# Norm, residual and norm before and after a feed forward: whole width or two halves of 256 tokens

## The chip, the core and the metric

The kernel is one program on one core of one Trainium2 chip. Its engines are TensorE (PE; weight loads are PEld), VectorE (DVE), ScalarE (ACT), GpSimd (POOL) and SyncE (SP, which issues DMAs). They run their own instruction streams in order and meet only at semaphores. The metric is the device time of one execution in microseconds (us), lower is better.

## The reference, cut to what matters

Two transformer-like blocks work on 512 tokens of width 1024. What the change touches is the end of the first block and the start of the second:

```python
def rmsnorm(x, g):
    ms = jnp.mean(xf * xf, axis=-1, keepdims=True)
    return (xf * lax.rsqrt(ms + EPS) * g)
...
    h = h + rmsnorm(mixed @ w_out[l], g_mix_post[l])      # border 1, first norm and residual
    hn = rmsnorm(h, g_ffn_pre[l])                         # border 1, second norm
    f = jnp.square(jax.nn.relu(hn @ w_ff1[l])) @ w_ff2[l] # the feed forward
    h = h + rmsnorm(f, g_ffn_post[l])                     # border 2, first norm and residual
...
    h = rmsnorm_2(x, norm1_g[l]) * (1.0 + sc1) + sh1      # border 2, second norm
    z = h @ w_in[l]                                       # conv_in ("cin"), latents, gates
```

Everything is float32 and each token is normed by itself, so a border can be done for some tokens ahead of the others.

## The kernel before, in words

Activations lie transposed: the partition is a channel and the free dimension holds the tokens, so a tile of width 1024 is 8 rows of 128x512. A matmul with float32 accuracy is made of three float32r ones: operands are split into a high part (an ACT copy that rounds) and a low part (a subtraction), and `three` (line 338) multiplies high by high, high by low and low by high. Weights are streamed in units of 128x2048 through a ring. For each unit ACT writes the high part (`high`, line 821) and DVE or POOL the low part (`low`, line 1339) into one of two places of `wsplit`; `high` of a unit waits until the unit two before it is used up. The order of units is the list PLAN, written out by hand; POOL_LOW says whose low part is POOL's. `next_high` and `next_low` handle the unit after the one named.

`linear` (line 346) does one unit: two output tiles of 128x512, each 8 rows of the input by three matmuls, 24 in all, into one of 8 PSUM banks. Units in the order of the program: "wo" 0 to 3 (w_out, tiles 0 to 7), then "f1" 0 to 7 and "f2" 8 units, twice over, with "ada" units between them that DVE alone works on, then "cin" 0 to 3, "lat", "ga", "gc" and so on. An f2 tile sums over two units.

A border is done across all 512 tokens:

- while the last linear units run, ACT squares each output row (`block_out`, line 1051, or line 1109) and DVE sums the squares in `nrm[:, 2]` (`sums`, line 1679). PE sums over the partitions with a matmul by ones (`total`), ACT takes the root (line 847), DVE the reciprocal (line 1369) into `rs`.
- `residual` (line 1689): for each of 8 rows DVE multiplies by gain and rs (line 1697), and DVE (even rows, line 1701) or POOL (odd rows, line 2227) adds it to X. ACT squares each row of X (`squares_of_x`, line 1063), PE sums the squares with eight matmuls by ones; then again root and reciprocal.
- for each row DVE makes the value (line 1713, in border 2 line 1778), ACT the high part (line 1082, in border 2 line 1118, and for odd rows line 1120), DVE (even rows, lines 1719 and 1782) or POOL (odd rows, lines 2234 and 2239) the low part. `linear("f1", i, ..., each="h_split")` follows row by row.

After border 1, for each f1 tile ACT takes ReLU and square (lines 1094 and 1096), DVE the square again and the low part (lines 1756 and 1759), and DVE adds an ada unit into `adab` (line 1735) ahead of the next unit's low part. After border 2, tiles cin 0 to 3 are copied to `CA` and 4 to 7 go through a sigmoid (`conv_gate`). A causal convolution of 31 taps on DVE (`convolve`, lines 1796 and 1799) starts when cin tiles 4 and 5 are there.

## Time and profile before

| what | value |
|---|---|
| median of 3 runs | 2111.68 us (2108.8 to 2114.98) |
| the profiled execution's own time | 2114.34 us |
| its span in the profile | 2112.5 us |
| mean granted TensorE clock | 0.925 of 2.4 GHz |
| PE / DVE / ACT / POOL busy | 88% / 63% / 37% / 23% |

The profile gives for each engine what it was busy with and what ended the idle time before it. In a row of the timeline the first number is the start from the span's start, the second the duration (of all of the instructions, where several are merged); the arrow in brackets names what the engine had waited for.

### The profile page before, as it was taken

Reading aid. Unit: us, or ns where it says so; the run is one execution under the profiler, and the core shown is the slowest. Engines: PE = TensorE matmul, PEld = TensorE weight load, DVE = VectorE, ACT = ScalarE, POOL = GpSimd, SP = SyncE. Lnnn points to the kernel's source line nnn. Section 1 sums busy time; section 2 is a strip of 40 time slices with the busy share of each in tenths; the row PEclk is TensorE's granted clock in tenths of the full one; section 3 lists DMA queues with packets and bytes.
Section 4 is the critical chain, followed back from the end, with each engine's and each line's share of the span. In section 5 each row is a group of like instructions: output and inputs, shape, how many; then the busy total and the mean of one; then the engine's idle time right before and its main releaser. Section 6 shows DMA issues by size and latency. Waiting matters only on the chain. (4 is left out here: it accounts for less than half of the span.)

```text
span 2112.5 us, 21287 instructions
## 1 busy us (share of the span) xinstructions
PE 1849.6 (88%) x8780; PEld 1447.2 (69%) x8780; DVE 1330.5 (63%) x1664; ACT 779.2 (37%) x994; POOL 496.4 (23%) x417
## 2 busy tenths in 40 slices
PE   4999878789699999699999996998688897789985
PEld 3778756677697888477888784776554574677774
DVE  3235588879545343566235455798978565798995
ACT  3343334332003123343123223324246433666663
POOL 1030066767242000110000001433200000544440
PEclk8999887789899999899999997999889998899997
DMA  6121020002001223134334341221110111989893
GB/s 224 62 80 61 20 80 0 1 21 85 16 2 60 80 100 126 54 140 163 148 147 180 140 159 41 85 100 60 60 60 1 40 40 48 358 341 349 338 352 148
DMA packets 37329, 241.35 MB, mean 114 GB/s; under 512 B 4192, under 2 KB 4704, under 8 KB 10736
## 3 DMA queue, kind: packets, MB, share of 16 engines
q1 hardware_dynamic: 23984, 147.69, 18.9%
q0 software_dynamic: 13248, 92.30, 11.4%
q8 instruction: 69, 1.13, 0.2%
q14 instruction: 28, 0.23, 0.0%
HBM read 228.39 MB, written 11.58 MB: 114 GB/s over the span
## 5 line engine op out<-in xcount | busy, mean ns | idle before, releaser
L336 PE MATMUL bank<-h_high,wsplit 128*128 128x512 f32 x992 | 323.4, 405 | 25.6 <-POOL wsplit L1339 8.6
L1339 DVE TENSOR_TENSOR wsplit<-ring,wsplit 128x2048 fp32r<-128x2048 f32 x77 | 177.4, 2304 | 182.0 <-ACT wsplit L821 181.9
L821 ACT ACTIVATE wsplit<-ring 128x2048 fp32r<-128x2048 f32 x98 | 186.9, 1907 | 212.3 <-PE bank L336 188.3
L336 PEld LDWEIGHTS bank<-h_high,wsplit 128*128 128x128 f32 x992 | 190.3, 192 | 79.9 <-POOL wsplit L1339 9.5
L336 PE MATMUL bank<-xn_high,wsplit 128*128 128x512 f32 (+1 forms) x832 | 219.9, 352 | 27.0 <-DVE wal_low L1390 18.5
L336 PE MATMUL bank<-h_low,wsplit 128*128 128x512 f32 x496 | 199.5, 402 | 0.0
L336 PEld LDWEIGHTS bank<-xn_high,wsplit 128*128 128x128 f32 x832 | 148.3, 194 | 49.3 <-issue 19.9
L336 PE MATMUL bank<-f_high,wsplit 128*128 128x512 f32 x512 | 166.3, 405 | 4.4 <-DVE f_low L1759 4.4
L2227 POOL TENSOR_TENSOR x<-x,z 128x512 f32<-128x512 f32 x8 | 12.8, 1594 | 598.8 <-DVE z L1697 598.8
L336 PE MATMUL bank<-xn_low,wsplit 128*128 128x512 f32 (+1 forms) x416 | 145.6, 350 | 0.0
L1799 DVE SCALAR_TENSOR_TENSOR conv<-conv_in,vecs,conv 128x512 f32<-128x512 f32 x120 | 140.5, 1171 | 4.3
L2263 POOL DMA_INDIRECT ring<-in_wmoe,indices x42 | 84.1, 2002 | 219.7 <-DVE routing L1999 139.8
L1339 POOL TENSOR_TENSOR wsplit<-ring,wsplit 128x2048 fp32r<-128x2048 f32 x21 | 98.3, 4682 | 113.0 <-ACT wsplit L821 112.7
L336 PEld LDWEIGHTS bank<-f_high,wsplit 128*128 128x128 f32 x512 | 99.3, 194 | 29.3 <-DVE f_low L1759 5.2
L336 PEld LDWEIGHTS bank<-h_low,wsplit 128*128 128x128 f32 x496 | 95.6, 193 | 22.2 <-issue 0.2
L336 PE MATMUL bank<-states,d_re 128*32 128x64 f32 x512 | 91.3, 294 | 18.1 <-DVE states L1618 18.1
L336 PE MATMUL bank<-f_low,wsplit 128*128 128x512 f32 x256 | 103.7, 405 | 0.0
L336 PE MATMUL bank<-states,d_im 128*32 128x64 f32 x512 | 91.7, 295 | 0.0
L336 PE MATMUL bank<-parts,block_high 128*128 128x512 f32 x216 | 74.1, 426 | 18.4 <-DVE block_out L2081 18.4
L336 PEld LDWEIGHTS bank<-xn_low,wsplit 128*128 128x128 f32 x416 | 80.7, 194 | 10.8 <-issue 0.7
L336 PE MATMUL bank<-m_high,wsplit 128*128 128x512 f32 x256 | 81.3, 396 | 2.0 <-DVE m_low L1928 2.0
L336 PE MATMUL bank<-g_high,wsplit 128*128 128x512 f32 x256 | 80.8, 395 | 0.0
(465 smaller groups left out, 3890.2 us busy)
## 6 DMA issues: line engine op xcount, KB each, us to landing
ring<-in_W SPq DMA_DIRECT2D x122, 1024.0 KB, 4.8
xslot<-zeros SPq DMA_DIRECT2D x7, 516.0 KB, 5.0
block<-xslot SPq DMA_DIRECT2D x7, 516.0 KB, 11.0
yslot<-block_out SPq DMA_DIRECT2D x7, 512.0 KB
x_in<-in_xT SPq DMA_DIRECT2D x4, 528.0 KB, 7.4
x<-in_xT SPq DMA_DIRECT2D x2, 1024.0 KB, 6.2
out_y<-h_tokens SPq DMA_DIRECT2D x4, 512.0 KB, 2.6
bc<-in_bc SPq DMA_DIRECT2D x1, 1024.0 KB, 4.7
```

Of the source, the lines that this page charges most:

```text
L336: return g.matmul(o, l, r, start=first, stop=last_, skip_group_check=True)
L821: g.activation(wst[:, side(n), 0, :], ringt[:, n % RING, :], ACT.Copy).then_inc(*a.sig(("high", n)))
L1339: g.tensor_tensor(wst[:, side(n), 1, :], ringt[:, n % RING, :], hi, SUB).then_inc(*t.sig(("low", n), ("released", n)))
L1799: g.scalar_tensor_tensor(out=CO[:, c, :], in0=i, scalar=cw[:, c, k:k + 1], in1=CO[:, c, :], op0=MUL, op1=ADD).then_inc(*v.sig(("convolved",)))
L2227: g.tensor_tensor(X[:, k, :], X[:, k, :], Z[:, k, :], ADD).then_inc(*q.sig((name, "x", k)))
L2263: g.indirect_dma_start(slots[c % NS], None, wmoe, indexed(x)).then_inc(slot_landed[c % NS], 16)
```

## The change

Both borders are done for the tokens 0 to 255 (half 0) and then 256 to 511 (half 1).

- PE: the last unit before a border (wo 3, f2 15; f2 14 too) is done as four half tiles of 24 matmuls with 256 columns, in the order (6, half 0), (7, half 0), (6, half 1), then the ones matmuls that sum half 0's squares, then (7, half 1). Then the eight ones matmuls for X of half 0, the sum for half 1's first norm, and the first two units after the border (f1 0 and 1, cin 0 and 1) as four tiles for half 0 and four for half 1. The ones matmuls for X of half 1 stand between the rows of the fourth half tile.
- DVE and POOL share the rows otherwise: DVE does both operations of rows 0, 2, 4, 6 and 7, POOL both of rows 1, 3 and 5. For POOL's rows ACT multiplies by the gain beforehand (`pool_rows`). DVE's sum of squares ends at row 5; rows 6 and 7 go to ones matmuls of their own.
- ACT: between the second root of half 0 and half 0's high parts stand the squares of half 1's last tiles, `pool_rows`, the high part of the next weight unit and the first root of half 1.
- DVE: the low part of that weight unit stands between half 0 and half 1. The low part of cin 1 is now DVE's and no longer POOL's. In border 2 the last sums of half 1 (`last_sum(1)`) stand behind the residual of half 0.
- High parts of f1 2 and cin 2 stand behind what ACT does with all eight half tiles.
- The load of positions waits for all of border 2 (`h2_done`).

```diff
-POOL_LOW = {... + [("cin", i) for i in (1, 2, 3)]
+POOL_LOW = {... + [("cin", i) for i in (2, 3)]
...
+        HALF = (slice(0, 256), slice(256, 512))
+        DVE_ROWS, POOL_ROWS, ROWS_COME = (0, 2, 4, 6, 7), (1, 3, 5), (0, 1, 2, 3, 4, 6, 5, 7)
... PE
+            def tile_half(name, i, j, h, xh, xl, need, beside=None):
+                n = UNIT[name, i]
+                wh, wl = weights(n, 8, 2048)
+                m, c = slice(128 * j, 128 * j + 128), HALF[h]
+                p.wait_ge(*at("low", n))
+                b = fresh(name, 2 * i + j, h)[:, 0:256]
+                for s, k in enumerate(ROWS_COME):
+                    p.wait_ge(*at(*need(k, h)))
+                    t = three(b, wh[:, k, m], wl[:, k, m], xh[:, k, c], xl[:, k, c], s == 0, s == 7)
+                    if beside and s < 7:
+                        beside(s)
+                t.then_inc(*p.sig((name, 2 * i + j, h), ("used", n)))
...
+            def mean_square(after, name, h):
+                b = fresh(after, h)[:, 0:256]
+                p.wait_ge(*at(name + "_added", 5))
+                mm(b, ones, nrm[:, 2, HALF[h]], True, False)
+                for z in range(2):
+                    p.wait_ge(*at(name + "_square", 6 + z, h))
+                    t = mm(b, ones, nrm[:, z, HALF[h]], False, z == 1)
...
+            def border(after, name, pre, first, xh, xl, need):
+                for s in range(8):
+                    square_of_x(pre, 0, s)
+                mean_square(after, name, 1)
+                for j in range(4):
+                    tile_half(first, j // 2, j % 2, 0, xh, xl, need, (lambda s: square_of_x(pre, 1, s)) if j == 3 else None)
+                for j in range(4):
+                    tile_half(first, j // 2, j % 2, 1, xh, xl, need)
...
+            for j, h in ((0, 0), (1, 0), (0, 1)):
+                tile_half("wo", 3, j, h, mh, ml, split)
+            mean_square("mix_post", "wo", 0)
+            tile_half("wo", 3, 1, 1, mh, ml, split)
+            border("mix_post", "wo", "ffn_pre", "f1", hh, hl, lambda k, h: ("h_split", k, h))
... ACT
+            next_high("wo", 3)
+            root_table()
+            last_tiles(0)
+            half_root("mix_post", 0)
+            squares_of_x("ffn_pre", 0)
+            half_root("ffn_pre", 0)
+            last_tiles(1)
+            pool_rows("ffn_pre", Z, vec("g_ffn_pre"), 0)
+            next_high("f1", 0)
+            half_root("mix_post", 1)
+            h_high(0)
+            squares_of_x("ffn_pre", 1)
+            half_root("ffn_pre", 1)
+            pool_rows("ffn_pre", Z, vec("g_ffn_pre"), 1)
+            h_high(1)
+            g.activation(cact, vec("c_2"), ACT.Sigmoid).then_inc(*a.sig(("c_sig",)))
+            for h in range(2):
+                for j in range(4):
+                    ... ReLU and square of f1 tile j, half h, 256 columns each
+            next_high("f1", 1)
... DVE
+            def residual(name, after, gain, out, h):
+                v.wait_ge(*at("root", after, h))
+                g.reciprocal(rs[:, c], rs[:, c]).then_inc(*v.sig(("inverse", after, h)))
+                for k in DVE_ROWS:
+                    g.scalar_tensor_tensor(out=Z[:, k, c], in0=Z[:, k, c], scalar=gain[:, k:k + 1], in1=rs[:, c], op0=MUL, op1=MUL).then_inc(*v.sig())
+                    v.wait_ge(*v.own())
+                    g.tensor_tensor(X[:, k, c], X[:, k, c], Z[:, k, c], ADD).then_inc(*v.sig((name, "x", k, h)))
+            residual("ffn_pre", "mix_post", vec("g_mix_post"), "wo_out", 0)
+            scaled_half("ffn_pre", Z, vec("g_ffn_pre"), "h_value", "h_split", 0, h_low)
+            next_low("f1", 0)
+            residual("ffn_pre", "mix_post", vec("g_mix_post"), "wo_out", 1)
+            scaled_half("ffn_pre", Z, vec("g_ffn_pre"), "h_value", "h_split", 1, h_low)
...
+                    if hf == 0 and i == 0:
+                        ... low parts of f1 tiles 0 to 3, half 0 then half 1, 256 columns each
+                    elif hf == 0 and i == 1:
+                        pass
... POOL
+                for k in POOL_ROWS:
+                    g.tensor_tensor(Z[:, k, c], Z[:, k, c], rs[:, c], MUL).then_inc(*q.sig())
+                    q.wait_ge(*q.own())
+                    g.tensor_tensor(X[:, k, c], X[:, k, c], Z[:, k, c], ADD).then_inc(*q.sig((name, "x", k, h)))
... ACT, behind border 2
+            for h in range(2):
+                for j in range(4):
+                    a.wait_ge(*at("cin", j, h))
+                    g.activation(CA[:, j, HALF[h]], banks.at("cin", j, h)[:, 0:256], ACT.Copy).then_inc(*a.sig(("free", "cin", j, h), ("cin_out", j)))
             conv_gate(1)
... SP
-            s.wait_ge(*at("h2_split", 6))
+            s.wait_ge(*at("h2_done"))
```

Border 2 is written in the same way with "ffn_post", "attn_pre", cin, `h2_high` (Identity with a bias, and a second one for rows 1, 3 and 5) and `h2_low`.

## Rows read from the trace of the kernel before

**Rows 1.** The page's first part, busy time and share of the span.

```profile
PE 1849.6 (88%) x8780; PEld 1447.2 (69%) x8780; DVE 1330.5 (63%) x1664; ACT 779.2 (37%) x994; POOL 496.4 (23%) x417
```

**Rows 2.** Stretches: bounds, length, busy (x) of PE, PEld, DVE, ACT, POOL, clock, DMA.

```profile
870.70:899.10 28.40, 10.82 (x19) 3.38 (x18) 20.49 (x19) 10.15 (x16) 6.38 (x4) 0.74 0.00 0
899.10:904.50 5.40, 5.15 (x10) 3.11 (x11) 5.40 (x7) 1.95 (x4) 3.48 (x2) 0.50 0.00 2
...
920.00:1260.00 340.00, 335.62 (x1445) 270.69 (x1444) 159.00 (x123) 96.43 (x102) 0.00 (x0) 0.98 0.42 158
```

**Rows 3.** Timeline, border 1, from the last wo matmul to the residual.

```profile
870.33 0.40 PE L336 MATMUL bank<-m_high,wsplit 128*128 128x512 f32 x1
...
873.02 1.13 PE L336 MATMUL bank<-norm_tmp,cst 128*128 128x512 f32 x2 [2.30 <-DVE norm_tmp L1685]
...
874.19 0.69 ACT L847 ACTIVATE norm_tmp<-bank,cst 128x512 f32<-128x512 f32 x1 [0.59 <-PE bank L336]
874.98 3.35 DVE L1369 RECIPROCAL norm_tmp<-norm_tmp 128x512 f32<-128x512 f32 x1 [2.10 <-ACT norm_tmp L847]
...
879.83 1.41 DVE L1697 SCALAR_TENSOR_TENSOR z<-z,vecs,norm_tmp 128x512 f32<-128x512 f32 x2
...
880.65 1.70 POOL L2227 TENSOR_TENSOR x<-x,z 128x512 f32<-128x512 f32 x1 [204.22 <-DVE z L1697]
...
881.27 1.64 DVE L1701 TENSOR_TENSOR x<-x,z 128x512 f32<-128x512 f32 x1
...
889.64 1.26 POOL L2227 TENSOR_TENSOR x<-x,z 128x512 f32<-128x512 f32 x1 [1.29 <-DVE z L1697]
```

**Rows 4.** Groups by tile: durations min/median/max in ns of the border's 512-column instructions.

```profile
L1701 DVE TENSOR_TENSOR x<-x,z x8: 691/1636/1640, 879.2 to 1302.8; 128x512 f32<-128x512 f32 x8
L1118 ACT ACTIVATE h_high<-h,adat x8: 722/724/727, 1313.3 to 1323.2; 128x512 fp32r<-128x512 f32 x8
```

**Rows 5.** Timeline behind border 1: DVE's ada and low part, ACT's ReLU of tiles 2, 3.

```profile
918.01 2.35 DVE L1735 SCALAR_TENSOR_TENSOR ada_sum<-ring,small,ada_sum 128x2048 f32<-128x2048 f32 x1
920.27 2.28 DVE L1339 TENSOR_TENSOR wsplit<-ring,wsplit 128x2048 fp32r<-128x2048 f32 x1
...
921.64 0.60 ACT L1094 ACTIVATE norm_tmp<-bank 128x512 f32<-128x512 f32 x1 [2.53 <-PE bank L336]
927.24 0.60 ACT L1094 ACTIVATE norm_tmp<-bank 128x512 f32<-128x512 f32 x1 [4.33 <-PE bank L336]
```

**Rows 6.** Timeline, border 2: last f2 matmul, POOL's low part, ACT's copy of cin 3, next high part.

```profile
1286.11 0.40 PE L336 MATMUL bank<-f_high,wsplit 128*128 128x512 f32 x1
...
1328.04 4.87 POOL L1339 TENSOR_TENSOR wsplit<-ring,wsplit 128x2048 fp32r<-128x2048 f32 x1 [1.82 <-ACT wsplit L821]
...
1344.47 0.60 ACT L1128 ACTIVATE conv<-bank 128x512 f32<-128x512 f32 x1 [5.00 <-PE bank L336]
1348.57 1.90 ACT L821 ACTIVATE wsplit<-ring 128x2048 fp32r<-128x2048 f32 x1
```

**Rows 7.** The chain that ended last, behind border 2: start, length, what.

```profile
1332.97 22.68 PE bank L336 x96
```

**Rows 8.** Half-size relatives elsewhere in the kernel: durations min/median/max in ns.

```profile
L1305 ACT ACTIVATE hidden<-bank x28: 385/385/388, 1821.5 to 2082.5; 128x256 f32<-128x256 f32 x28
L2071 DVE TENSOR_TENSOR hidden<-hidden,bank x28: 420/420/423, 1822.9 to 2083.3; 128x256 f32<-128x256 f32 x28
L1353 POOL TENSOR_TENSOR pool_products<-powers,bc x48: 702/748/1150, 291.4 to 622.4; 128x288 f32<-128x288 f32 x48
```

**Rows 9.** Timeline, matmuls with 264 columns, first and last of 26 like them.

```profile
45.03 0.28 PE L336 MATMUL bank<-xn_low,wsplit 128*128 128x264 f32 x1
...
54.15 0.29 PE L336 MATMUL bank<-xn_low,wsplit 128*128 128x264 f32 x1
```

**Rows 10.** Timeline, DVE and POOL working beside each other on 288 columns.

```profile
290.86 1.72 DVE L1357 TENSOR_TENSOR d_re<-products 64x288 f32<-64x288 f32 x2
...
292.35 1.90 POOL L1357 TENSOR_TENSOR d_re<-pool_products 64x288 f32<-64x288 f32 x2
```

More of the change, by code:

```diff
@@ L604, in tensor, with total @@
             p.end("end", "ffn", "pe")
-            total("ffn_post", nrm[:, 2, :], ("ffn_squares",))
-            squares_of_x("attn_pre")
+            border("ffn_post", "ffn", "attn_pre", "cin", hh2, hl2, lambda k, h: ("h2_split", k, h))
             hb = [(0, hh2, hl2)]
-            for i in range(4):
-                linear("cin", i, hb, each="h2_split")
+            for i in range(2, 4):
+                linear("cin", i, hb)
+            def total(name, a, *need):
+                b = fresh(name)
+                for w in need:
+                    p.wait_ge(*at(*w))
+                mm(b, ones, a, True, True).then_inc(*p.sig((name,)))
+                banks.close(name)
             for i in range(3):
@@ L1051, in block_out, with pool_rows @@
+            def pool_rows(name, to, gain, h):
+                c = HALF[h]
+                for k in POOL_ROWS:
+                    a.wait_ge(*at(name, "x", k, h))
+                    g.activation(to[:, k, c], X[:, k, c], ACT.Copy, scale=gain[:, k:k + 1]).then_inc(*a.sig((name, "gained", k, h)))
+            a.wait_ge(*at("end", "glu", "pe"))
+            a.wait_ge(*at("end", "glu", "dve"))
+            for i in range(3):
+                next_high("wo", i)
                 for j in (2 * i, 2 * i + 1):
-                    a.wait_ge(*at(name, j, 0))
@@ L1076, in scalar @@
-            root_table()
-            root(("mix_post",), rs, 1024, 512)
-            squares_of_x("ffn_pre")
-            a.wait_ge(*at("end", "wo", "pe"))
-            for k in range(8):
-                a.wait_ge(*at("h_value", k))
-                g.activation(hh[:, k, :], Z[:, k, :], ACT.Copy).then_inc(*a.sig(("h_high", k)))
-            g.activation(cact, vec("c_2"), ACT.Sigmoid).then_inc(*a.sig(("c_sig",)))
+                        a.wait_ge(*at("wo_added", j - 2))
+                    b = banks.at("wo", j, 0)
@@ L1084, in scalar @@
+            next_high("f1", 1)
             for hf in range(2):
-                for i in range(8):
+                for i in range(0 if hf else 2, 8):
                     next_high("f1", 8 * hf + i)
@@ new lines, in scaled_half @@
+            def scaled_half(name, o, gain, value, split, h, low_of):
+                c = HALF[h]
+                v.wait_ge(*at("root", name, h))
+                g.reciprocal(rs[:, c], rs[:, c]).then_inc(*v.sig(("inverse", name, h)))
+                v.wait_ge(*v.own())
+                g.scalar_tensor_tensor(out=o[:, 0, c], in0=X[:, 0, c], scalar=gain[:, 0:1], in1=rs[:, c], op0=MUL, op1=MUL).then_inc(*v.sig((value, 0, h)))
+                for k, after in zip(DVE_ROWS, DVE_ROWS[1:] + (None,)):
+                    if after:
+                        g.scalar_tensor_tensor(out=o[:, after, c], in0=X[:, after, c], scalar=gain[:, after:after + 1], in1=rs[:, c],
+                                               op0=MUL, op1=MUL).then_inc(*v.sig((value, after, h)))
+                    low_of(k, c, split, h)
@@ new lines, in scaled_half, with value_of @@
+            def scaled_half(name, o, hi, lo, value, high_, split, h):
+                c = HALF[h]
+                def value_of(k):
+                    q.wait_ge(*at("inverse", name, h))
+                    q.wait_ge(*at(name, "gained", k, h))
+                    q.wait_ge(*q.own())
+                    g.tensor_tensor(o[:, k, c], o[:, k, c], rs[:, c], MUL).then_inc(*q.sig((value, k, h)))
+                value_of(POOL_ROWS[0])
+                for k, after in zip(POOL_ROWS, POOL_ROWS[1:] + (None,)):
+                    if after:
+                        value_of(after)
+                    q.wait_ge(*at(high_, k, h))
+                    q.wait_ge(*q.own())
+                    g.tensor_tensor(lo[:, k, c], o[:, k, c], hi[:, k, c].bitcast(F32), SUB).then_inc(*q.sig((split, k, h)))
```

266 lines of the change are left out of this document (158 added, 108 removed).

## The prediction

> **What bounds the kernel now.** I read the busy shares first: PE is busy 88% of the span, more than any other engine [rows 1], so time is lost where PE stands. The view by stretches shows two such places, alike. Between the feed forward's ends PE works 335.6 of 340 us, so nothing is to be gained there; in border 1 it works only 10.8 of 28.4 us, on the ones matmuls of the norms, and then 5.4 us at a granted clock of 0.50, 1.2 of 2.4 GHz, behind the splits [rows 2]. The timeline says what goes on meanwhile: a reciprocal of 3.35 us, twice, and rows that DVE and POOL pass between them [rows 3]. Counted to a full rate, border 1 costs this: wo's last matmul ends at 870.7, tiles 2 and 3 are 5.6 us apart, and f1 tile 3 ends at 927.2 [rows 3, 5]; that is 56.5 us for four tiles of 5.6, so 34 are lost. Border 2 runs from 1286.5 to cin tile 3 at 1344.4 [rows 6], 57.9 us, 35.5 lost. What comes behind hangs on PE in both cases: behind border 1 the feed forward, behind border 2 the chain goes through four PE tiles, 96 matmuls [rows 7], to DVE's convolution. So what counts is when unit f1 2, and when unit cin 2, can begin. Before, f1 2 begins at 927.2 and cin 2 at 1344.4.
>
> I count from the start of the last unit before a border, two tiles of 5.6 us ahead of its end: 859.5 and 1275.3. On that clock f1 2 begins at 67.7 and cin 2 at 69.1.
>
> **Prices at half width.** A matmul with 264 columns comes every 0.1216 us (75 in 9.12) [rows 9], so 256 columns take 0.118 and a half tile of 24 takes 2.83, half a full one: PE pays nothing for halving. ACT takes 0.385 from a bank [rows 8]; the step from 512 to 256 columns is 0.21, from 0.60 [rows 6]. So an Identity goes from 0.724 to 0.51 and a root from 0.69 to 0.48 [rows 3, 4]; copies and squares from memory lie between, I take 0.42. DVE pays 0.42 for a tensor-tensor [rows 8] against 0.69 [rows 4] and 0.70 for its products [rows 3], so two halves cost 0.15 more than the whole each time; with the gap to the next I take 0.45. A reciprocal halves to about 1.75. A ones matmul goes from 1.13 to 0.57 [rows 3]. POOL takes 0.70 for 288 columns and 1.26 for 512 [rows 3, 8], so 0.62 for 256.
>
> The price that decides is that of DVE and POOL together. DVE's addition takes 0.69 at best but 1.64 in the median [rows 4], POOL's 1.26 alone and 1.70 beside DVE [rows 3]. In the timeline POOL's ends 1.11 us behind DVE's product (881.24 to 882.35), and DVE's addition 0.56 behind POOL's end (882.91) [rows 3]: they take turns, and only their starts overlap. For 288 columns beside each other DVE needs 0.86 and POOL 0.95 for one [rows 10], about 0.9 a pair; for 256 I take 0.8. The ends of this price: 0 for the wait, when DVE alone sets the pace, and the full sum of 0.45 and 0.62, 1.07. The row with 288 columns is the nearest, so it decides.
>
> One phase (residual, or value and split) has ten DVE and six POOL instructions: the first DVE one 0.5, six pairs 4.8, three DVE ones left 1.4, together **6.7 us** for a half. Before, the residual of all 8 rows ran from the reciprocal's end at 878.3 to POOL's last addition at 890.9, 12.6 us [rows 3]; twice 6.7 is 13.4. Halving thus makes the border's own work longer; it is the cover by PE that must pay.
>
> The Trainium skill, SBUF — State Buffer, Who interferes with whom, speaks against this more strongly: there the later of the two blocks until the other's whole instruction is over. The rows above show a shorter exclusion. By its rule the sum below would lie about 11 us higher.
>
> **Border 1, step by step.** Three half tiles 8.5; three ones matmuls 1.7 (10.2); root 0.5 (10.7); reciprocal 1.75 (12.45); residual of half 0 6.7 (19.15); last square, ones matmul, root 1.5 (20.65). Now ACT, not DVE, is late: four operations on the last tiles 1.6, three gains 1.3, the high part of f1 1 1.9 [rows 6], root 0.5, and the first high part 0.4 (26.4), while DVE's reciprocal is done at 22.4. Then DVE has eight instructions left and POOL four: four pairs 3.2 and four alone 1.8 (31.4). Half 1 follows: low part of f1 1 2.3 [rows 5] (33.7), reciprocal 1.75, residual 6.7 (42.15), square, ones, root 1.5, reciprocal 1.75 (45.4), values and splits 6.7 (52.1), last row's matmuls 0.4 (52.5), three half tiles 8.5 (61.0). The four tiles of half 0 lie inside (31.8 to 43). Here a **new wait** opens: the high part of f1 2 no longer runs beside the tiles, it stands behind all eight ReLUs, and DVE has an ada unit before its low part. ReLU and square 0.9, DVE's low part of the tile 0.4, ada 2.35, low part 2.3 [rows 5]: f1 2 begins at 67.0. ACT's backlog of half 0 tiles (from 52.5, with the sigmoid's table) is gone by about 60, just in time. Against 67.7 the gain is **0.7 us**.
>
> The moved sums of squares cost nothing on the path; they hide beside the half tiles of the last unit, and without that cover would cost 0.4 to 0.7 each.
>
> **Border 2.** The same to 20.65; ACT's part is squares 0.85, gains 1.3, high part 1.9, root 0.5 (25.2), then eleven Identities of 0.51 (30.8) and the last low 0.5 (31.3), so ACT binds there. `last_sum(1)` on DVE (0.85) lies beside ACT's squares. Then 2.3, 1.75, 6.7, 1.5, 1.75 and 6.7 (52.0), 0.4 and 8.5 (60.9). Behind it stand the copy of tile 3 (0.4), the high part of cin 2 (1.9) and POOL's low part at 4.87 [rows 6], less 0.1 when nothing contends: cin 2 begins at 68.0 against 69.1, gain **1.1 us**. Taking cin 1's low part from POOL spares nothing more; before, it ended at 1332.91 just ahead of the tiles that needed it, at 1332.97 [rows 6, 7], and ahead of the convolution. The position load is later, but DVE then has over 10 us until tiles 4 and 5 for it. SP's weight loads move with the use of their units and have one ring of lead.
>
> Sum: 0.7 + 1.1 = 1.8 us off. Of the profiled execution, 2114.34 us (span 2112.5), that leaves 2112.5; the median of the runs lies 2.7 lower, so I forecast **2109.9 us**. 0.3%, 6.3 us, is about what a measurement of this kernel can tell from no change.
>
> **Rivals.**
> - *The two engines overlap more than taken.* If DVE's own pace (4.7 a phase) sets it, border 1 gains three times 2.0 and 1.4, border 2 three times 2.0: 13.4 more, 2096.5. For: POOL has fewer, shorter instructions, and DVE runs one-input work too. Against: [rows 10]. Chance 0.22.
> - *PE's half clock falls on the path* (the other side). Behind border 1 PE ran 5.4 us at 0.50, after an idle stretch, where ten matmuls of 512 columns filled 5.15 us [rows 2]; before, that was hidden behind the splits. Now three tiles of half 1 stand behind the last split, with nothing beside them. At half clock a 256-column matmul streams 256 / 1.2 GHz = 0.213, so each takes 5.1 instead of 2.83: 7 us a border, 14 in all, 2123.9. It decides as soon as more than 3 us a border are slow. For: an idle of about 3 us before half 1's splits, and row-wise matmuls that fill PE partly. Against: behind border 1 such row-wise matmuls brought the clock back, for the ReLUs of tiles 2 and 3 are 5.6 us apart [rows 5]. Chance 0.12. The Trainium skill, TensorE: Matmul & The Clock Gate, What's actually happening, has the same rule, that the array is throttled by default and activity releases it.
> - *Turns by whole instructions.* A pair costs 1.07 instead of 0.8: 22 pairs in border 1 and 18 in border 2 on the path, 10.8 us more, 2120.7. For: medians of 1.64 and 1.70. Against: the 0.56 and 1.11 above. Chance 0.08. This is the SBUF page's rule of the Trainium skill.
> - *A wait not seen*, in a program with so many new semaphores: 0.05.
>
> **How the numbers follow.** The forecast case has 0.53 and its own range is 2104 to 2117, from handoffs of 0.04 us (sum's end at 874.15 to the root at 874.19 [rows 3]) at some twenty steps a border and 0.1 a pair either way. About 0.05 of it falls under 2105.4 and 0.03 over 2118. Faster: 0.22 + 0.05 = 0.27; slower: 0.12 + 0.05 of the third rival + 0.03 of the last + 0.03 of the case = 0.23; within 0.3%: 0.50. The range reaches most of the way to both sides: 2098 to 2122.
>
> **What would show it.** In the profile after, residual and value phases of about 6.7 us with DVE and POOL in turns; about 4 us between the second reciprocal of half 0 and its first low part, with ACT busy; PE idle for about 6 us between the last half tile and f1 2, and 7 before cin 2; the feed forward between unchanged. I'd be wrong if phases took 5 us or 8, if the half 1 tiles took over 3 us each, if f1 2 began well ahead of its place, or if the convolution did not move with cin 2.

## The result, and the profile after

The changed kernel takes **2122.1 us** (median of 5, 2121.0 to 2124.1) where the kernel before took 2113.4 beside it: a ratio of 1.0041 [1.0027, 1.0056]. It is slower by 9 us, and in later runs again: 1.0060 [1.0045, 1.0075]. The forecast was 2109.9, a small gain. The profiled execution took 2122.0 us with a span of 2120.2, 7.7 more than before.

Four marks that both kernels have cut the span into comparable pieces: ACT's first read of wo tile 5 (the last unit before border 1 starts there), ACT's ReLU of f1 tile 4 (the first tile of unit f1 2), DVE's last modulation sum (just ahead of border 2), and ACT's sigmoid of cin tile 5 (the last of unit cin 2). A modulation sum is what follows a group of ada units, three times in the feed forward: PE sums `adab` over the partitions with sixteen matmuls of one output column each, and DVE adds the result into `adat`. The timeline of the kernel before, by start, length, engine and what ended the idle time ahead of it:

```profile
859.56 0.60 ACT L1053 ACTIVATE z<-bank 128x512 f32<-128x512 f32 x1 [4.28 <-PE bank L336]
...
932.84 0.60 ACT L1094 ACTIVATE norm_tmp<-bank 128x512 f32<-128x512 f32 x1 [2.53 <-PE bank L336]
...
1273.85 0.17 DVE L1742 TENSOR_TENSOR adat<-bank,vecs 128x16 f32<-128x16 f32 x1 [8.11 <-PE bank L336]
...
1355.67 0.60 ACT L1131 ACTIVATE conv_in<-bank 128x512 f32<-128x512 f32 x1 [3.29 <-PE bank L336]
```

The same four of the changed kernel:

```profile
859.52 0.60 ACT L1144 ACTIVATE norm_tmp<-bank 128x512 f32<-128x512 f32 x1 [4.51 <-PE bank L339]
...
935.57 0.60 ACT L1200 ACTIVATE norm_tmp<-bank 128x512 f32<-128x512 f32 x1 [3.31 <-PE bank L339]
...
1279.37 0.17 DVE L1887 TENSOR_TENSOR adat<-bank,vecs 128x16 f32<-128x16 f32 x1 [9.27 <-PE bank L339]
...
1367.07 0.60 ACT L1262 ACTIVATE conv_in<-bank 128x512 f32<-128x512 f32 x1 [5.00 <-PE bank L339]
```

So border 1 takes 76.05 us instead of 73.28 (+2.8), the feed forward behind it 343.8 instead of 341.0 (+2.8), border 2 87.7 instead of 81.8 (+5.9); behind it 3.7 come back (753.1 against 756.8), which makes the 7.7.

The waits that the prediction announced are there. PE's waits from 871 to 928 and from 1291 to 1354 (what ended them; us in total, times, longest):

```profile
PE bank L339 <- DVE h_low L1848: 8.5, 2, 4.6
PE bank L339 <- DVE wsplit L1471: 5.9, 1, 5.9
...
PE bank L339 <- DVE h_low L1852: 8.2, 2, 4.7
PE bank L339 <- POOL wsplit L1471: 6.9, 1, 6.9
```

5.9 us for DVE's low part of f1 2 and 6.9 for POOL's of cin 2. The chain that ended last goes through them, from half 1's last tiles to the convolution:

```profile
1333.49 12.65 PE bank L339 x87
...
1346.16 0.38 ACT conv L1267
1346.54 1.81 ACT wsplit L882
...
1348.48 4.51 POOL wsplit L1471
...
1353.04 14.01 PE bank L339 x48
```

The last line is the surprise: 48 matmuls are two tiles, 11.2 us at full rate, and they take 14.0. The view by stretches says why (bounds, length, PE busy, granted clock, DMA share, GB/s). Border 1, where [rows 2] had its stretches before:

```profile
871.00:899.00 28.00, 20.75 (x119) 0.88 0.00 1
899.00:905.00 6.00, 4.46 (x28) 1.00 0.00 0
905.00:913.00 8.00, 4.81 (x23) 0.79 0.01 2
913.00:922.00 9.00, 8.87 (x75) 1.00 0.59 233
922.00:928.00 6.00, 0.21 (x1) 0.76 0.23 66
928.00:940.00 12.00, 12.00 (x44) 0.83 0.83 318
```

and border 2:

```profile
1291.00:1312.00 21.00, 14.38 (x64) 0.81 0.00 0
...
1335.00:1346.00 11.00, 11.00 (x82) 0.86 0.38 121
1346.00:1353.00 7.00, 0.12 (x2) 0.67 0.00 0
1353.00:1359.00 6.00, 5.96 (x15) 0.53 0.49 175
```

While PE stands for the weights of f1 2 or cin 2, the granted clock falls toward 0.50, 1.2 of 2.4 GHz, and the tile behind the wait starts there: 0.53 over 1353 to 1359. Before, nothing stood at these places: f1 2's high part ran beside the tiles, and ACT read f1 2's first tile 5.6 us behind the last of f1 1 (927.24 in [rows 5], 932.84 in the first list above).

### The profile page after: what moved, and what is told of

The parts are those of the page before. It is cut to its first block, busy times and chain, and to the rows that moved or that the text cites. A ratio compares the mean times of both kernels' runs of the same rounds, so it can differ in the third digit from the quotient of the medians.

```text
span 2120.2 us, 22234 instructions
## 1 busy us (share of the span) xinstructions
PE 1862.0 (88%) x9168; PEld 1489.4 (70%) x9168; DVE 1333.0 (63%) x1707; ACT 792.5 (37%) x1065; POOL 505.1 (24%) x448
## 4 chain that ended last, share of the span: by engine, by line
PE 65%; DVE 26%; ACT 5%; issue 3%; DMA 1%; POOL 1%; SPq 0%; POOLq 0%; DVEq 0%; ACTq 0%
PE bank L339 64%; DVE conv L1961 7%; DVE u_shuffled L1722 2%; DVE states L1750 1%; DVE products L1745 1%; DVE wsplit L1471 1%; DVE states L1748 1%; DVE wsplit L2209 1%; DVE products L1746 1%; DVE parts L2209 1%; DVE qk L1501 1%; DVE norm_tmp L1501 1%; ACT wsplit L882 1%; ACT parts L1414 1%; ACT probs_t L1333 0%
## 5 line engine op out<-in xcount | busy, mean ns | idle before, releaser
L339 PE MATMUL bank<-h_high,wsplit 128*128 128x512 f32 (+1 forms) x1120 | 342.6, 388 | 39.3 <-POOL wsplit L1471 15.1
L339 PEld LDWEIGHTS bank<-h_high,wsplit 128*128 128x128 f32 x1120 | 215.1, 199 | 85.2 <-POOL wsplit L1471 15.7
L339 PE MATMUL bank<-h_low,wsplit 128*128 128x512 f32 (+1 forms) x560 | 214.0, 382 | 0.0
L339 PE MATMUL bank<-f_high,wsplit 128*128 128x512 f32 (+1 forms) x576 | 170.2, 381 | 4.4 <-DVE f_low L1924 4.4
L2393 POOL TENSOR_TENSOR z<-z,norm_tmp 128x256 f32<-128x256 f32 x12 | 9.2, 767 | 586.1 <-DVE norm_tmp L1824 585.2
L2444 POOL DMA_INDIRECT ring<-in_wmoe,indices x42 | 85.5, 2036 | 218.9 <-DVE routing L2161 136.4
L339 PEld LDWEIGHTS bank<-h_low,wsplit 128*128 128x128 f32 x560 | 112.1, 200 | 20.7 <-issue 0.2
L339 PEld LDWEIGHTS bank<-f_high,wsplit 128*128 128x128 f32 x576 | 107.9, 195 | 26.4 <-DVE f_low L1924 5.2
L1471 POOL TENSOR_TENSOR wsplit<-ring,wsplit 128x2048 fp32r<-128x2048 f32 x20 | 93.7, 4686 | 120.7 <-ACT wsplit L882 120.3
L339 PE MATMUL bank<-f_low,wsplit 128*128 128x512 f32 (+1 forms) x288 | 109.3, 380 | 0.0
L339 PE MATMUL bank<-parts,block_high 128*128 128x512 f32 x216 | 73.8, 425 | 18.4 <-DVE block_out L2243 18.4
L339 PE MATMUL bank<-m_high,wsplit 128*128 128x512 f32 (+1 forms) x288 | 83.1, 372 | 2.0 <-DVE m_low L2090 2.0
```

Of the source, the lines that this page charges most:

```text
L339: return g.matmul(o, l, r, start=first, stop=last_, skip_group_check=True)
L1471: g.tensor_tensor(wst[:, side(n), 1, :], ringt[:, n % RING, :], hi, SUB).then_inc(*t.sig(("low", n), ("released", n)))
L2444: g.indirect_dma_start(slots[c % NS], None, wmoe, indexed(x)).then_inc(slot_landed[c % NS], 16)
```

## The experiments

Each kernel was timed against the kernel before on the same chip. **Theory A**, from the profile: the halves work as forecast, and each border loses by its new wait and by PE's half clock behind it. **Theory B**: the halves themselves (shorter instructions, fixed costs, turns of DVE and POOL) cost it. Measured, in the pieces above (wo 5 to f1 4, f1 4 to the last modulation sum, that to cin 5, the rest of the span), from the one profiled execution of each:

| kernel | ratio to before, 95% | border 1 | feed forward | border 2 | rest |
|---|---|---|---|---|---|
| before | 1 | 73.3 | 341.0 | 81.8 | 756.8 |
| changed | 1.0041 [1.0027, 1.0056] | 76.1 | 343.8 | 87.7 | 753.1 |
| after_again | 1.0060 [1.0045, 1.0075] | 76.2 | 343.7 | 87.8 | 753.2 |
| b1only | 1.0025 [1.0015, 1.0035] | 76.2 | 343.4 | 82.6 | 751.6 |
| warm | 1.0024 [1.0011, 1.0038] | 74.2 | 342.1 | 85.5 | 751.8 |
| warm_all | 1.0026 [1.0014, 1.0037] | 74.2 | 342.2 | 84.4 | 753.2 |
| warm_more | 1.0013 [1.0003, 1.0023] | 74.2 | 342.2 | 83.0 | 757.7 |
| ada_warm | 1.0038 [1.0025, 1.0052] | 76.0 | 343.9 | 84.4 | 753.1 |
| before_warm | 0.9995 [0.9984, 1.0005] | 73.2 | 338.1 | 84.1 | 753.7 |
| early_f1 | 1.0011 [0.9998, 1.0024] | 70.3 | 342.1 | 87.9 | 753.4 |
| early_cin | 1.0004 [0.9991, 1.0016] | 76.1 | 343.8 | 78.0 | 754.7 |
| early_both | 0.9993 [0.9982, 1.0004] | 71.9 | 343.0 | 78.5 | 755.7 |
| mid_high | 0.9959 [0.9945, 0.9972] | 71.3 | 340.0 | 78.2 | 757.0 |
| mid_high2 | 0.9956 [0.9941, 0.9971] | 70.0 | 338.5 | 78.1 | 753.6 |
| best | 0.9980 [0.9968, 0.9992] | 70.2 | 341.3 | 77.2 | 751.7 |
| best2 | 0.9976 [0.9966, 0.9986] | 71.6 | 339.9 | 78.2 | 759.5 |
| best_warm | 0.9956 [0.9938, 0.9974] | 69.3 | 339.4 | 74.1 | 753.7 |
| mid_high_warm | 0.9946 [0.9932, 0.9961] | 69.2 | 343.7 | 76.1 | 754.7 |

Besides changed and after_again, two pairs are the same code (mid_high and mid_high2, best and best2): their borders differ by up to 1.5 us and their rest by up to 7.8. A difference of the rest is therefore not read as an effect, and one of 1.5 us in a single border only where several kernels repeat it: the five that keep the changed border 1 agree there to 0.2 us (76.0 to 76.2), and the three warm ones to 0.1 (74.2).

### Is it the clock behind the waits? (warm)

Nothing is moved; matmuls whose sums nobody reads are put into PE's two waits.

```diff
+            def warm(name, x, now, then, n):
+                b = fresh(name)
+                for k in range(now):
+                    mm(b, x[:, 0:128], x, True, True)
+                p.wait_ge(*at("high", n))
+                for k in range(then):
+                    t = mm(b, x[:, 0:128], x, True, True)
...
+                        if hf == 0 and i == 2:
+                            warm("warm1", hh[:, 0, :], 8, 8, UNIT["f1", 2])
...
+            warm("warm2", hh2[:, 0, :], 8, 10, UNIT["cin", 2])
             for i in range(2, 4):
                 linear("cin", i, hb)
```

> Matmuls whose sums nobody reads are put into PE's two new waits of the changed kernel: 8 of 512 columns right behind the last half tile of f1 0/1 and 8 more behind the high part of f1 2, and 8 and 10 in the same places before cin 2. All waits stay. Theory A (each wait costs its length of 6 and 7 us, and then PE's half clock costs again, for the first tile behind the wait takes 7.8 and 8.4 us where a tile takes 5.6): f1 2 and cin 2 begin where they do in the changed kernel, 927.7 and 1353.0 on its clock, but their first tiles take about 5.6 us; 2.2 + 2.8 = 5.0 us less than the changed kernel, about 2117. Theory B (the phases of DVE and POOL at half width are what costs; PE's clock behind the wait is hidden or chance): no change, 2122, within 1 us. If the added matmuls run at half clock themselves they take 6.9 and 7.7 us, end up to 1 us late, and the gain shrinks to 3.

It took 1.9 us off border 1 and 2.2 off border 2; the ratio of 1.0024 stands against 1.0041 and 1.0060 of the changed kernel. That is 4.1 us where 5.0 were expected, in the direction that only theory A allows. Part of what is missing is in the expectation: at the full clock the first tile behind such a wait takes 5.9 us from its first matmul to ACT's read (929.09 to 934.99 and 1351.09 to 1356.99 in warm), not 5.6, so of the 7.8 and 8.4 us of the changed kernel 1.9 and 2.5 are the clock's. The stretches of the kernel warm over its two waits and the tiles behind them:

```profile
922.00:928.00 6.00, 5.13 (x26) 1.00 0.16 59
928.00:934.00 6.00, 4.92 (x22) 1.00 0.92 352
...
1345.00:1351.00 6.00, 3.53 (x15) 1.00 0.00 0
1351.00:1357.00 6.00, 5.91 (x25) 1.00 0.49 175
```

1.00 throughout, where the changed kernel had 0.76 and 0.83, 0.67 and 0.53. From ACT's read of the last half tile to the first matmul of f1 2 are 5.88 us, 5.89 in the changed kernel; only the clock differs. The unread matmuls did not fill the wait for cin 2 to its end:

```profile
1351.09 0.50 PE L339 MATMUL bank<-h_high,wsplit 128*128 128x512 f32 x1 [2.14 <-POOL wsplit L1484]
```

### Take the waits away (early_f1, early_cin, early_both)

```diff
             for h in range(2):
+                if h:
+                    next_high("f1", 1)
                 for j in range(4):
...
-            next_high("f1", 1)
...
+                            if h:
+                                ada_begin(UNIT["f1", 1] + 1)
+                                next_low("f1", 1)
```

> Border 1 alone: ACT makes the high part of f1 2 ahead of half 1's ReLUs, and DVE the ada unit and the low part of f1 2 ahead of half 1's low parts. The side of the split weights is free when f1 0 has its half 1 tiles, two half tiles (5.7 us) before f1 1 ends; high 1.9 and low 2.3 are 4.2, so they fit. Theory A: the wait of 6 us before f1 2 is gone, f1 2 begins at 921.8 to 922.5 instead of 927.7, and its first tile takes 5.6 to 6 instead of 7.8: 5.2 + 2.0 = 7.2 to 8.1 us less than the changed kernel, some of it given back at the ada matmuls, about 2115. Theory B (halving itself costs it, the handoffs behind the border are as good as hidden): less than 2 us less, since PE would then find another wait in the feed forward, 2120 or more.

Border 1 fell by 5.7 us, to 70.3, with a ratio of 1.0011. The expectation of 7.2 to 8.1 was too high for a reason that the profile shows: f1 2's weights were not there, and ACT stood 2.5 us for their transfer with half 1's ReLUs behind it. Their place in the ring is that of a modulation unit, which DVE reads only behind half 1's splits. The timeline of mid_high, which has the same order there (DVE frees the place at 914.8, SP's transfers start, and the high part can start at 919.64):

```profile
913.54 1.29 DVE L1877 TENSOR_SCALAR ada_sum<-ring,small 128x2048 f32<-128x2048 f32 x1
...
914.86 17.02 SPq L2476 DMA_DIRECT2D ring<-in_W  x6
...
919.64 1.92 ACT L882 ACTIVATE wsplit<-ring 128x2048 fp32r<-128x2048 f32 x1 [2.35 <-DMA ring<-in_W]
```

The same for border 2:

```diff
-POOL_LOW = {UNIT[p] for p in [("zg", i) for i in range(4)] + [("zs", 0), ("zs", 1)] + [("cin", i) for i in (2, 3)]
+POOL_LOW = {UNIT[p] for p in [("zg", i) for i in range(4)] + [("zs", 0), ("zs", 1)] + [("cin", 3)]
...
+                    if h and j == 2:
+                        next_high("cin", 1)
                     a.wait_ge(*at("cin", j, h))
...
             g.tensor_scalar(PR, PR, PI_IN, -PI_IN, ALU.min, MAX).then_inc(*v.sig(("angles",)))
+            next_low("cin", 1)
```

> Border 2 alone: the high part of cin 2 is made between half 1's second and third copies, and its low part on DVE (2.3 us) behind the position angles instead of on POOL (4.5). High at 1340.3 to 1342.2, DVE's angles end at 1342.8, low until 1345.1, the last half tile ends at 1346.1 on the changed kernel's clock. Theory A: cin 2 begins at 1346.1 instead of 1353.0 and its first tile takes 5.6 instead of 8.4: DVE's convolution moves up by 6.9 + 2.8 = 9.7 us; behind it up to a third is given back, as the 11 us lost in the changed kernel shrank to about 8: 2113 to 2115. Theory B: the tiles of half 1 are the loss and a wait ahead of the sigmoid's part stays: under 3 us, 2119 or more.

Border 2 took 78.0, 9.7 under the changed kernel, just as expected, and the kernel is level with the one before (1.0004). ACT makes the high part between two copies, DVE the low part behind the angles, and both are done before the last half tile:

```profile
1339.03 1.91 ACT L882 ACTIVATE wsplit<-ring 128x2048 fp32r<-128x2048 f32 x1
...
1341.00 2.29 DVE L1470 TENSOR_TENSOR wsplit<-ring,wsplit 128x2048 fp32r<-128x2048 f32 x1
...
1344.43 0.39 ACT L1267 ACTIVATE conv<-bank 128x256 f32<-128x256 f32 x1 [2.45 <-PE bank L339]
```

Both together:

> The early splits of f1 2 and of cin 2 together, without those of f1 1 and cin 1. Alone they took 0.30% and 0.37% off the changed kernel (1.0011 and 1.0004 against 1.0041). If the two borders add: 0.67%, a ratio of 0.9974, 5.5 us under the kernel before. Theory B (the halves themselves cost what the changed kernel lost): it cannot go below 1.0000, as a border of two halves would be no shorter than before. What mid_high had beyond this, 0.9959 against 0.9974, is then the worth of the first units' early splits: 3 us, not the 6 hoped for.

71.9 and 78.5 in the borders, within 1.6 and 0.5 us of their own runs. The ratio, 0.9993 [0.9982, 1.0004], misses the 0.9974 expected, so it doesn't refute theory B by itself. The borders speak against it: both are shorter than the whole ones before (73.3, 81.8), border 2 by 3.3 us, which is more than two profiles of one program differ by, border 1 by 1.4, which is not. What refutes it is mid_high, below.

### One border alone, and the changed kernel again (b1only, after_again)

b1only takes the changed code for border 1 and the kernel before for border 2, line for line.

> The change at border 1 alone; border 2 and the units beside it as in the kernel before. In the changed kernel the high parts of the middle of the feed forward are 2.7 us late, and the last modulation sum ahead of border 2 is 5.5 us late. Theory A (each border loses by its own new wait and the clock behind it): 2.7 to 5.5 us above the kernel before, a ratio of 1.0013 to 1.0026, and border 2 takes as long as it did. Theory C (the loss is one of border 2, the late start in the feed forward is made up): under 1 us, a ratio of 1.0005 or less. Theory D (the shift of 2.8 us between 1156 and 1279 in the changed kernel was chance of the clock): the shift at 1279 is 2.7 us, not 5.5.

> The changed kernel, unaltered, beside the others on this chip, so that their ratios to the kernel before stand beside its own. Every theory: the ratio of 1.0041 again, within 0.0015.

1.0025 [1.0015, 1.0035], 5.3 us, inside what theory A said: in the profile border 1 costs 2.9 in itself and 2.4 in the feed forward, and border 2 takes 82.6, nearly what it did (81.8). So theory C (a loss of border 2 alone) falls, and theory D too, as the longer feed forward comes with border 1's code. Every kernel with border 1 and the feed forward unaltered has 343.4 to 343.8 there. after_again lies 0.0019 above 1.0041, where 0.0015 was expected at most; the two intervals overlap, so the loss is known as 0.4 to 0.6%.

### What the halves cost with the clock kept up (warm_all, warm_more, before_warm)

warm_all puts unread matmuls also before the half tiles of each half:

```diff
                 mean_square(after, name, 1)
+                warm(pre + "_warm0", wst[:, side(n0), 0, 0:512], (("high", n0), 0), (("root", pre, 0), 8), ((value, 0, 0), 4))
                 for j in range(4):
                     tile_half(first, ...)
+                warm(pre + "_warm1", wst[:, side(n0), 0, 0:512], (("root", pre, 1), 8), ((value, 0, 1), 4))
```

> The changed kernel with unread matmuls in all six waits of the two borders: those of the kernel warm (in front of f1 2 and cin 2), and 8 of 512 columns behind the second root of each half, 4 more behind its first value, so that PE does not stand before the half tiles either. Theory A: in border 2 of the changed kernel the half tiles of half 0 held up the ones matmuls (1.4 us) and the half tiles of half 1 ran at 0.63 to 0.68 for 10 us; both gone, border 2 from the last modulation sum to cin tile 5 takes 87.7 - 2.8 - 1.4 - 1.5 = 82 us, and border 1 (73.3 us before, 76.1 changed, 74.2 in warm) takes 73.5 to 74; the whole 3 us under warm, a ratio of 1.0010. Theory B: no less than warm, 1.0024 or more.

A miss: 84.4 in border 2, not 82, and 1.0026, which by itself is what theory B said (1.0024 or more). Half 1's last tile indeed ended 2.4 us sooner behind the first root (52.6 us, 1286.80 to 1339.35, against 54.9), but PE stood 2.13 us before cin 2, and the clock was 0.65 from 1348 to 1352:

```profile
1341.58 2.58 PE L339 MATMUL bank<-h_high 128*128 128x512 f32 x10 [0.43 <-ACT wsplit L898]
1346.30 0.49 PE L339 MATMUL bank<-h_high,wsplit 128*128 128x512 f32 x1 [2.13 <-POOL wsplit L1487]
```

The kernel warm had the same gap of 2.14 us and 1.00 behind it, so the gap alone doesn't decide; what else does, no run here shows. warm_more bridges it:

```diff
-                            warm("warm1", hh[:, 0, :], (None, 8), (("high", UNIT["f1", 2]), 8))
+                            warm("warm1", hh[:, 0, :], (None, 8), (("high", UNIT["f1", 2]), 12))
...
-            warm("warm2", hh2[:, 0, :], (None, 8), (("high", UNIT["cin", 2]), 10))
+            warm("warm2", hh2[:, 0, :], (None, 8), (("high", UNIT["cin", 2]), 18))
```

> warm_all with 12 instead of 8 unread matmuls behind the high part of f1 2 and 18 instead of 10 behind that of cin 2, so that PE works until POOL's low part ends. In warm_all border 2, from the last modulation sum to cin tile 5, took 84.4 us and its first tile behind the wait 1.5 us more than 5.6. Theory A: 82.9 us here (81.8 in the kernel before), border 1 as in warm_all (74.2 against 73.3); the ratio 1.0018 where warm_all had 1.0026. What is left, 0.9 and 1.1 us, is the halves' own price, not the clock's.

83.0 and 74.2, and 1.0013. With the clock at 1.00 through the tiles of half 1 and of cin 2, the two borders cost 0.9 and 1.1 us more than whole rows. So by these profiles 6.6 of the 8.7 us lost in the two borders go with the clock; the 2.1 left are the halves together with their two new waits, which still stand here. The 1.1 is no larger than the spread of border 2 (81.8 and 82.6 for the same code, in before and b1only); the 0.9 repeats in all three warm kernels.

before_warm puts them into the kernel before, behind the sums of squares of each border:

```diff
             squares_of_x("ffn_pre")
+            warm("warm1", wst[:, side(n0), 0, 0:512], (("high", n0), 8), (("root", "ffn_pre"), 8), (("h_value", 0), 6))
```

> The kernel before with unread matmuls in the two waits behind the squares (8, 8 and 6 of 512 columns). If the half clock was hidden there behind the splits, as the forecast had it: f1 tile 2 and cin tile 2 begin no sooner, border 1 takes 73.3 and border 2 81.8 us as before, ratio 1.0000 within 0.0010. If it was not hidden: 1 to 3 us less a border, 0.9975.

The clock did rise. The stretch 896 to 904, before and in before_warm:

```profile
896.00:904.00 8.00, 4.65 (x10) 0.50 0.00 1
...
896.00:904.00 8.00, 5.32 (x18) 1.00 0.00 1
```

So it did from 1312 to 1322 (0.50 before, 1.00 here). Yet the ratio is 0.9995 and border 1 73.2: before, the half clock cost nothing in border 1. In the two pieces behind it, the last modulation sum came 2.9 us sooner and border 2 took 84.1, 2.3 more than expected; their sum is the same to 0.6 (422.2 against 422.8).

### The feed forward (ada_warm)

The stretches around the second and third modulation sum, before:

```profile
1152.00:1160.00 8.00, 8.00 (x31) 0.79 0.62 235
1272.00:1280.00 8.00, 8.00 (x36) 0.79 0.32 117
```

and in the changed kernel:

```profile
1152.00:1160.00 8.00, 8.00 (x39) 0.61 0.11 27
1276.00:1284.00 8.00, 8.00 (x44) 0.57 0.13 36
```

PE works without a pause there, but on matmuls of one column, and the clock falls behind them, in both kernels and for longer in the changed one. The whole 2.8 us of the feed forward arise at these two places: from f1 tile 4 to the first sum both kernels take 91.4 us, from there to the second 128.3 and 129.5, to the third 121.3 and 122.9. ada_warm puts an unread matmul of 512 columns behind every fourth of them.

```diff
                         for j in range(16):
                             t = mm(b[:, j:j + 1], adab[:, 128 * j:128 * j + 128], ones[:, 0:1], True, True)
+                            if j % 4 == 3:
+                                u = mm(w, fh[:, 0, 0:128], fh[:, 0, :], True, True)
```

> The changed kernel with an unread matmul of 512 columns behind every fourth of the sixteen one-column matmuls of each modulation sum, 12 in all, which cost 2.8 us by themselves. In the changed kernel PE is granted 0.50 for some 4 to 6 us behind each of the three sums. Theory A (those stretches are PE's answer to the one-column matmuls, and their length is what differs between the kernels): the feed forward from the ReLU of f1 tile 4 to the last sum takes 338 to 341 us instead of 343.8. Rival: the unread matmuls are too few to hold the clock, then 346. The whole: 2 to 5 us under the changed kernel, or 3 over it.

343.9 up to the last sum, where neither theory A (338 to 341) nor the rival (346) has it, and 3.3 us less in border 2's piece, which begins inside the last slow stretch; the ratio, 1.0038, is that of the changed kernel's first runs (1.0041), and its interval overlaps that of the later ones (1.0060) too, so a gain of 2 to 5 us for the whole is not shown. Around the third sum the clock was 1.00 instead of 0.62 (1275 to 1282), around the second 0.72 instead of 0.50 (1154 to 1160). So the unread matmuls do raise the clock, and seem to cost about what they bring: twelve are an estimated 3 us (ten take 2.58 in the row of warm_all above). That the slow stretches are the clock's is shown; why their length differs between kernels with the same feed forward is left open. It differs even between profiles of one program (340.0 and 338.5 for mid_high, 341.3 and 339.9 for best).

### Versions that beat both (mid_high, best, best_warm, mid_high_warm)

mid_high is early_both, and makes the split of the second unit (f1 1, cin 1) ahead of half 0 instead of between the halves:

```diff
             half_root("mix_post", 0)
+            next_high("f1", 0)
             squares_of_x("ffn_pre", 0)
...
-            next_high("f1", 0)
...
+            next_low("f1", 0)
             scaled_half("ffn_pre", Z, vec("g_ffn_pre"), "h_value", "h_split", 0, h_low)
-            next_low("f1", 0)
```

> Both changes of the two kernels beside it (the splits of f1 2 and cin 2 made early), and also those of f1 1 and cin 1: the high part before the squares of half 0, the low part before the values of half 0, where DVE stands for the root. Theory A: both waits and the half clock behind them gone is about 16 us less than the changed kernel, less a third given back behind border 2, 2106 to 2108 by that alone; the weights of the second unit taken out of ACT's block (1.9) and out of DVE between the halves (2.3 less 0.8) are up to 3 more a border, 2100 to 2105 together. Theory B: not below 2116.

2103.0 us where the kernel before had 2110.2: 0.9959 [0.9945, 0.9972], well past what theory B allows.

best moves f1 2's splits behind two of half 1's ReLUs:

```diff
             for h in range(2):
-                if h:
-                    next_high("f1", 1)
                 for j in range(4):
+                    if h and j == 2:
+                        next_high("f1", 1)
```

> mid_high with the splits of f1 2 two half tiles later on ACT and DVE. In mid_high ACT stood 2.35 us for f1 2's weights, whose slot of the ring the unit before it frees only at 914.8; they landed at 919.6, and all ReLUs of half 1 stood behind that. Now two of them come first. If ACT's backlog held PE up: f1 2 starts 1 us sooner and the ratio is 0.9954; if f1 2 waits for its low part, which comes no sooner than its weights, no change: 0.9959, within 0.0010.

> best again, to stand beside mid_high on one chip (0.9980 and 0.9959 were taken on two). Both 3 to 8 us under the kernel before; between themselves 0 to 1 us, best the faster.

> mid_high again, beside best: 0 to 1 us above it, a ratio of 0.9960 to 0.9980.

best was to be level with mid_high or up to 1 us faster, and is slower both times (0.9980 and 0.9976 against 0.9959 and 0.9956; of the second pair, on one chip, the medians are 2106.6 and 2103.8 us). The intervals still touch, so the size is uncertain. Its borders are not longer, and the runs don't say what is. mid_high2, expected at 0.9960 to 0.9980, repeats mid_high.

best_warm and mid_high_warm are these two with warm_all's unread matmuls before the half tiles (the diff above, without those in front of f1 2 and cin 2):

> best with unread matmuls before the half tiles of each half (four places, 12 of 512 columns each). In best PE is granted 0.60 and 0.71 after half 0's wait and 0.67 after half 1's in border 1, 0.52 to 0.79 in border 2. Theory A: what lies on the path of it is some 1 us in border 1 and 2 us in border 2: 2 to 3 us under best. If the added matmuls end later than the splits they stand before: up to 1 us over best.

> mid_high (0.9959 and 0.9956 of the kernel before) with the unread matmuls of best_warm, which brought best from 0.9976 to 0.9956. If they add: 0.9936, 13 us under the kernel before. If both reach the same end by two ways (mid_high had already the better phase of the clock): 0.9956.

best_warm gained 4 us on best by the ratios (0.9956 [0.9938, 0.9974] against 0.9976 [0.9966, 0.9986]) and 7 by the medians (2099.5 against 2106.6), where 2 to 3 were expected; the intervals overlap, so the gain is likely and its size not settled. mid_high_warm has the lowest ratio, 0.9946 [0.9932, 0.9961], halfway between the two values expected, and its interval holds both 0.9936 and mid_high's own 0.9956 and 0.9959: whether the unread matmuls help mid_high as a whole is not shown. Its borders are 1 to 2 us shorter each than mid_high's, and its feed forward is at 343.7 again. The clock over the two borders of mid_high_warm:

```profile
871.00:928.00 57.00, 48.92 (x284) 1.00 0.21 76
1291.00:1346.00 55.00, 49.81 (x293) 0.99 0.14 44
```

## Why the prediction was wrong, step by step

**What held.** The prices at half width: a reciprocal of 1.75, and a pair of DVE and POOL on 256 columns. The residual of half 0:

```profile
869.44 0.47 ACT L1116 ACTIVATE norm_tmp<-bank,cst 128x256 f32<-128x256 f32 x1 [3.24 <-PE bank L339]
...
869.95 1.75 DVE L1824 RECIPROCAL norm_tmp<-norm_tmp 128x256 f32<-128x256 f32 x1 [5.05 <-ACT norm_tmp L1116]
...
871.74 0.48 DVE L1830 SCALAR_TENSOR_TENSOR z<-z,vecs,norm_tmp 128x256 f32<-128x256 f32 x1
...
873.01 0.94 DVE L1830 SCALAR_TENSOR_TENSOR z<-z,vecs,norm_tmp 128x256 f32<-128x256 f32 x1
...
873.81 0.73 POOL L2393 TENSOR_TENSOR z<-z,norm_tmp 128x256 f32<-128x256 f32 x1
...
874.62 0.79 POOL L2395 TENSOR_TENSOR x<-x,z 128x256 f32<-128x256 f32 x1
874.74 0.94 DVE L1830 SCALAR_TENSOR_TENSOR z<-z,vecs,norm_tmp 128x256 f32<-128x256 f32 x1
```

Two pairs every 1.73 us (873.01 to 874.74), 0.87 for one where 0.8 was taken, and the phase 7.0 us (871.7 to 878.7) where 6.7 was. Half 0's splits end 20.9 us behind the start of the first root, forecast 21.2. The rival that the two engines overlap falls: DVE alone would do one in 0.45 (0.48 for the first product, 0.42 to 0.43 for additions with POOL at rest). So does that of whole turns, 0.45 and 0.73 (POOL's shortest here), 1.2. The Trainium skill, SBUF — State Buffer, Who interferes with whom, has an exclusive lock there, by which the later one is blocked for the other's whole instruction. These rows don't agree: a pair takes 0.87, less than the sum of the two.

**Border 1.** The step "Square, ones, root 1.5" of half 1 took 2.6: DVE's last addition ends at 901.35 and the root starts at 903.49. The sums of squares stand between the matmuls of half 0's last tile, one behind every three, and PE was late with them:

```profile
901.53 0.47 PE L339 MATMUL bank<-h_high,wsplit 128*128 128x256 f32 x1
...
902.32 0.47 PE L339 MATMUL bank<-h_high,wsplit 128*128 128x256 f32 x1
...
902.86 0.59 PE L339 MATMUL bank<-norm_tmp,cst 128*128 128x256 f32 x2
```

A round takes 0.79 (901.53 to 902.32), and a row's sum stands at the end of its round. "The moved sums of squares cost nothing on the path" was wrong by 1.1 us a border. It isn't the clock: in warm_all the root of half 1 starts as late behind ACT's last squares as here (1.69 us, 1.70 here). Half 0's own step, with no tiles between its sums, took 1.7, so 0.9 of the 1.1 is the interleaving. From half 1's second root to ACT's read of the last half tile are 18.4 us, forecast 17.8. The wait of 5.9 was forecast as 6.0. So f1 2 begins at 68.3 on the prediction's clock (927.79), 1.3 behind the forecast of 67.0, instead of 0.7 ahead of the kernel before 0.6 behind it.

**The step that failed most** is one that the sum did not have: it ended at the start of f1 2 and of cin 2, so a tile behind the new wait was left at 5.6 like any other. It took 7.8, 2.2 more, from the first matmul behind the wait to the mark at 935.57:

```profile
927.79 0.80 PE L339 MATMUL bank<-h_high,wsplit 128*128 128x512 f32 x1 [5.92 <-DVE wsplit L1471]
```

cin 2's first took 8.4 (1353.04 to 1361.47), 2.8 more. Of the 2.2 and 2.8, 0.3 each is the start behind a wait, as in warm, and 1.9 and 2.5 are the clock's. The second rival had the mechanism, PE's half clock on the path, but put it at half 1's tiles and at 7 us a border. In border 1 half 1's first half tile did run at half clock (0.79 over 905 to 913), but beside the splits, and it cost nothing: from the root to the last half tile warm_more takes 18.4 us too. In border 2 it cost 1.5.

**Border 2**, counted from the first root's start (1291.23): half 1's root comes 34.9 us behind it, forecast 32.95, of which some 1.1 is again the sums between the matmuls and the rest PE's slow half tiles of half 0 (with the clock kept up in warm_all it is 33.9); the last half tile is read 20.1 behind that, forecast 17.8, where warm_all with a full clock has 18.6. The wait is 6.9 as forecast (7.1). With -1.1 for the gain that was expected: -1.1 + 1.9 + 2.3 - 0.2 + 2.8 = 5.7, measured 5.9. For border 1: -0.7 + 1.3 + 2.2 = 2.8, measured 2.8.

**The feed forward between** was to be unchanged, and lost 2.8 more, at its second and third modulation sum, where the clock stays down longer behind one-column matmuls; why longer is open. Behind border 2, 3.7 came back, which no row here explains and which is within what one program differs there. [rows 2] showed PE in the feed forward as busy 335.6 of 340 us; a busy share says nothing of the rate.

The range ended at 2122.0 because the clock's rival was worked out as a sum of 14 us with a chance of 0.12. What spoke for it was in [rows 2], 5.4 us at 0.50 behind an idle stretch; the prediction named that row, and still did not lay it beside the waits of 6 and 7 us that it had itself forecast. The Trainium skill, TensorE: Matmul & The Clock Gate, HAM oscillation — how this bites in real kernels, describes waits that put PE back to the low clock each time. The trace agrees, by 0.83 and 0.53 behind the two waits and 1.00 in the kernel warm.

## What to carry to other kernels

Where a change opens a new wait of several microseconds in front of PE, price it twice: its length, and the first tile behind it, which starts at half clock (here 2.2 and 2.8 us more behind waits of 5.9 and 6.9). A stage cut in halves for overlap should have the next unit's weights split before its last half, or the handoff behind the border can take back what the overlap gave; with the splits moved ahead, the same halves won 0.4% here (mid_high) instead of losing it. An order of operations that looks free on a slack engine, as sums put between matmuls, can be late by a round or more of what it is put between (here 1.1 us at rounds of 0.79).

## What was not expected of the hardware

Without a pause in PE's records the clock fell to 0.50 behind the one-column matmuls of the modulation, and 0.72 and 1.00 came back with four matmuls of 512 columns among each sixteen. Matmuls that nobody reads, put into PE's waits, took 1.9 and 2.2 us off the changed kernel's borders, and did nothing for the kernel before (0.9995), though they raised its clock from 0.50 to 1.00 there, because other work hid the half clock. A gap of 2.1 us that they left before cin 2 had 1.00 behind it in one kernel (warm) and 0.65 in another (warm_all). And one program's profiled executions differed by 7.8 us behind border 2 (751.7 and 759.5), with the same instructions, so single spans of this kernel are no measure of a change of 0.3%.
